# Decoder layer, up-projection by a seven-product scheme: two value buffers, norm weights moved from the weight tiles to the input's splits, sums of the first tile made in place in product order

## The chip, the cores and the metric

The kernel runs on one core of a Trainium2 chip. The metric is the device time of one execution in microseconds (us). The engines are TensorE (PE, with its weight loads as PEld), VectorE (DVE), ScalarE (ACT), GpSimd (POOL) and SyncE (SP, which here only issues DMAs). Each engine runs its own instructions in program order, and engines wait for one another on semaphores.

## What is computed

One layer of a hybrid decoder on 1040 prompt rows and 8 decode rows, all in float32. The change touches the end of the attention half (`h = x + mixed @ w_merge`) and the first half of the channel mixer:

```python
def rms_norm(x, w):
    y = xf * lax.rsqrt(jnp.mean(xf * xf, axis=-1, keepdims=True) + EPS)
    return (y * w.astype(jnp.float32)).astype(x.dtype)
...
    h = x + mixed @ w_merge
    hn = rms_norm(h, ffn_norm_w)
    g, val = jnp.split(hn @ w_up, [D_FF], axis=-1)
    g_hist = jnp.concatenate([ffn_prev.astype(x.dtype), g], axis=1)
    g_conv = causal_dwconv(g_hist, ffn_conv_w) + ffn_conv_b
    y = h + (jax.nn.silu(g_conv) * val) @ w_down
```

D_MODEL is 1024 and D_FF is 2816, so `w_up` is worked off in 22 tiles of 128 gate columns and 128 value columns.

## The kernel before

**Three products for one.** A float32 operand is split into a high part (ACT rounds a copy to float32r) and a low part (the rest, by a subtraction on DVE or POOL). Each product is high x high, high x low and low x high on TensorE.

**Seven products for eight.** For one tile of 128 gate and 128 value columns, `w_up` has four blocks of 512 x 128 (g1, g2, v1, v2) and the activations `h` have four blocks (upper or lower 512 features, first or second 520 columns). `sums` on DVE makes four sums of weight blocks (SW0 to SW3), and seven products P1 to P7 (24 matmuls of 260 columns each) stand for the eight block products. P1, P2 and P4 use g1, g2 and v2; P5, P6, P7 and P3 use SW0 to SW3. The activation side has B11 and B2 (blocks of `h`), T1, T2, T3 and T4 (their sums and differences), each with a high and a low part. These seven operands are made once, before and during the first tile, and serve all 22 tiles.

**One tile.** Tiles are numbered (i, a), a = 0 or 1; the loop runs over i, so two tiles per turn, and the first and the last ones are written out. After the first tile, TensorE takes the products in the order P1, P5, P6, P2, P7, P3, P4. P1, P6, P7 and P4 add up in one PSUM buffer (`MAIN[a]`), P2 stands in the other one, P5 and P3 in a third (`PXX`). After P1, P6, P5 and P4, ACT copies a half of a gate or value tile out of PSUM (copies G1, G2, V2, V1), and DVE adds the rest (adds G1, G2, V2). So P6 waits for copy G1, P7 for copy G2, P3 for copy V2, P4 for add V2, and the next tile's P1 and P5 for adds G1 and G2.

**What else goes on per tile.** DVE multiplies the two raw weight tiles by the norm weight (`scale`, twice), makes the four weight sums, multiplies the gate by the row norm RB (`gates`), does the width-3 convolution of the tile before (`conv`: two long instructions and three of 8 columns for the decode rows) and the last product with the value tile (`times_val`). ACT makes the high parts of the weights for the next tile (`high`), the first term of the convolution (`gate_half`), `silu`, and issues the store of the finished tile (`put_away`). POOL makes the low parts (`low`) and multiplies by the row norm (`times_rms`). SP loads the raw tiles RAWG and RAWV.

**One value buffer.** V serves all tiles. So copy V2 of a tile comes behind `put_away` of the tile before, and that waits for `times_val` on DVE, which reads the old V.

**The first tile** (`first_up` on TensorE, order P1, P2, P5, P3, P6, P7, P4) begins while its operands are still being made: DVE makes T3F, T2F, T4F for four feature groups kk after the merge is over, ACT rounds them, DVE makes the low parts of T2 and POOL those of T3 and T4. RB comes from a sum over rows on TensorE, three square roots on ACT and one `reciprocal` on DVE.

**Code order.** No scheduler is at work: each engine's order is the order in which its block is written. What the change moves is moved by hand.

Of the kernel before, what the change touches and what calls it, by code (L numbers as in the profile page):

```python
# [29 lines left out]
P = 128  # L30
# [13 lines left out]
YW = 344  # L44
# [50 lines left out]
def build(nc, io):  # L95
    ctx = ExitStack()
    with ctx:
# [116 lines left out]
        def parts(name, shape, high, low):  # L214
# [13 lines left out]
        T1F, T2F, T3F, T4F = (at(f"T{j}F", half, o) for j, o in (  # L228
            (1, oh1 + 3 * HB), (2, o7 + HB), (3, o7 + 3 * HB), (4, o7 + 5 * HB)))
# [5 lines left out]
        V = at("V", [P, NP], o1)  # L235
# [15 lines left out]
        HY = at("HY", [P, KD, NC], oh1 + 4 * HB)  # L251
# [118 lines left out]
        SUMS = {"P1": 1, "P2": 1, "P4": 2, "P5": 3, "P6": 4, "P7": 5, "P3": 6}  # L370
# [8 lines left out]
        def copied(i, a, what):  # L379

            order = ("G1", "V2", "G2", "V1") if is_first(i, a) else ("G1", "G2", "V2", "V1")
            return 22 + 4 * (2 * i + a) + order.index(what) + 1

        def added(i, a, what):

            return 21 + 3 * (2 * i + a) + ("G1", "V2", "G2").index(what) + 1

# [17 lines left out]
        def _(sp):  # L405
# [181 lines left out]

            sp.wait_ge(mm[1], place(NF // 2 - 1, 1, "P1"))
            activations(0, 0)
            down_weights(0)  # L590
            sp.wait_ge(mm[1], place(NF // 2 - 1, 1, "P7"))
            activations(1, 1)
            sp.wait_ge(mm[1], place(NF // 2 - 1, 1, "P3"))
            for m in range(KD):
                sp.dma_start(HY[:, m, :], hx_d[m, :, :]).then_inc(x_in[m], 16)
# [17 lines left out]
            for m in range(KD):  # L613
                sp.wait_ge(d_px, 24 * (NF // 2 - 1) + NCH * (m + 1))
                sp.dma_start(io["y"][:, m, :], HY[:, m, Y0:NC]).then_inc(out_done, 16)
# [7 lines left out]
        def _(pe):  # L623
# [424 lines left out]
            def first_up():  # L1048
# [10 lines left out]
                pe.wait_ge(n_rt, 5)  # L1059
# [10 lines left out]
                pe.wait_ge(n_lop, 12)  # L1070
# [51 lines left out]
        def _(act):  # L1122
# [413 lines left out]
            for m in range(8):  # L1536
                if m < 7:
                    hi(m % 2, 26 + m // 2)
                act.wait_ge(h_out, m + 1)
                if m >= 2:  # L1540
                    act.wait_ge(n_acc, KD + m - 2)
                nc.scalar.activation((HACC if m == 0 else HSQ)[:, :], HX[:, m, :], ACT.Square).then_inc(n_sq, 1)
                if m < 4:
                    nc.scalar.copy(B11[0][:, m, :], HX[:, m, 0:HALF]).then_inc(n_hi, 1)
                    act.wait_ge(n_t, KD + m + 1)
                    nc.scalar.copy(T1[0][:, m, :], T1F[:, m, :]).then_inc(n_hi, 1)
                else:
                    nc.scalar.copy(B2[0][:, m - 4, :], HX[:, m, :]).then_inc(n_hi, 1)
                act.dma_start(hx_d[m, :, :], HX[:, m, 0:NC]).then_inc(x_in[m], 16)
# [32 lines left out]
            def t_high(j, kk):  # L1582
                act.wait_ge(n_t, 12 + 3 * kk + (3, 2, 4).index(j) + 1)
                nc.scalar.copy((T2, T3, T4)[j - 2][0][:, kk, :], (T2F, T3F, T4F)[j - 2][:, kk, :]).then_inc(n_hi, 1)

            act.wait_ge(mm[0], 30)
            high(0, 0, "P5")
            copy(0, 0, "G1")
# [27 lines left out]
            def up(i, a, last=False):  # L1616
# [21 lines left out]
                copy(i, a, "V2")  # L1638
# [44 lines left out]
        def _(pool):  # L1683
# [187 lines left out]
            for p in ("P1", "P2", "P5", "P3"):  # L1871
                low(0, 0, p)
            for kk in range(4):
                t_low(3, kk)
# [605 lines left out]
```

## Time and profile before

| | us |
|---|---|
| median of 3 runs | 1815.49 (1811.84 to 1821.8) |
| the profiled execution | 1801.86 |
| its span | 1800.0 |
| end of the merge to first matmul of the up-projection | about 1032.5 to 1033.85 |
| up-projection's 22 tiles on TensorE | 1033.85 to about 1541 |
| down-projection | to the end |

The span is the time between the first and the last recorded instruction; the execution adds 1.86 us around it. The three timed runs lie 10 to 20 us above the profiled execution, so durations are read from the profile and the difference is put onto the median. A tile of the up-projection is found in the timeline by its matmuls on line 1043: `WP3H` is the weight of product P3, and so on.

### The profile page before, as it was taken

The page shows a single profiled execution, that of the slowest core. Times are in us where ns is not written, and L with a number is a line of the kernel's source. Part 1 is how long each engine was busy: PE and PEld are TensorE (multiplying, and loading weights), DVE is VectorE, ACT ScalarE, POOL GpSimd, SP SyncE. Part 2 cuts the span into 40 slices and gives each one's busy share as a digit, 9 for nine tenths or more (in the row PEclk, how much of TensorE's full clock was granted, in tenths as well). Part 3 has the DMA queues.
Part 4 walks back from the last instruction along what each step waited for, and adds up shares of the span by engine and source line. Part 5 has one row for each costly group of instructions (what it writes and reads, how often), then busy time and mean ns, then how long its engine had stood idle before and what let it go on. Part 6 is the DMA issues. An engine that isn't in the chain of part 4 may idle for free.

```text
span 1800.0 us, 32034 instructions
## 1 busy us (share of the span) xinstructions
PE 1689.1 (94%) x11519; PEld 1620.4 (90%) x11519; DVE 1303.0 (72%) x1988; ACT 687.3 (38%) x1049; POOL 902.2 (50%) x479
## 2 busy tenths in 40 slices
PE   7999999999999899998999968999999999999999
PEld 5868999999999798887999968999999999899999
DVE  5569999999899566555443398888888887555555
ACT  4755551322112477774112243333333334311110
POOL 2505751554876476662221267665666556544441
PEclk9999999999999799999999989999999999999999
DMA  5321112113775332222433212112222211622222
GB/s 192 85 64 36 47 40 91 56 51 116 255 229 193 106 89 83 83 95 83 137 123 141 98 56 71 70 70 71 73 76 77 75 72 62 244 94 94 94 75 94
DMA packets 66978, 178.32 MB, mean 99 GB/s; under 512 B 15386, under 2 KB 15514, under 8 KB 66762
## 3 DMA queue, kind: packets, MB, share of 16 engines
q1 hardware_dynamic: 56786, 140.91, 23.8%
q10 hardware_dynamic: 9392, 32.10, 4.7%
q0 software_dynamic: 720, 4.29, 0.6%
q8 instruction: 46, 0.75, 0.2%
q14 instruction: 34, 0.28, 0.1%
HBM read 141.79 MB, written 35.58 MB: 99 GB/s over the span
## 4 chain that ended last, share of the span: by engine, by line
PE 59%; DVE 24%; issue 7%; ACT 4%; POOL 3%; DMA 1%; SPq 1%; DVEq 1%; ACTq 1%; POOLq 0%
PE PS L634 16%; PE PX L1108 14%; PE PS L969 5%; PE PS L1014 4%; PE PX L1043 4%; PE PS L922 4%; DVE TG L2313 3%; DVE TG L2296 2%; PE PS L892 2%; DVE SW L2253 2%; DVE S L2067 2%; DVE M L2065 2%; PE PX L905 2%; PE PS L950 2%; DVE LD L2047 2%
## 5 line engine op out<-in xcount | busy, mean ns | idle before, releaser
L634 PE MATMUL PS<-XH,WHI 128*128 128x346 f32 (+1 forms) x984 | 321.2, 326 | 5.7 <-POOL WLO L1687 4.4
L634 PE MATMUL PS<-XL,WHI 128*128 128x346 f32 (+1 forms) x984 | 317.9, 323 | 0.0
L634 PE MATMUL PS<-XH,WLO 128*128 128x346 f32 (+1 forms) x984 | 317.3, 322 | 0.0
L1687 POOL TENSOR_TENSOR WLO<-WRAW,WHI 128x1024 fp32r<-128x1024 f32 x58 | 143.8, 2479 | 296.9 <-ACT WHI L1136 296.8
L2320 DVE TENSOR_TENSOR HY<-HY,PX 128x344 f32<-128x344 f32 x264 | 135.3, 513 | 114.0 <-PE PX L1108 114.0
L2067 DVE MATCH_REPLACE8 S<-M,S 128x1024 f32<-128x1024 f32 (+3 forms) x224 | 206.0, 926 | 0.0
L2065 DVE MAX8 M<-S 128x8 f32<-128x1024 f32 (+3 forms) x224 | 200.8, 932 | 0.4
L634 PEld LDWEIGHTS PS<-XH,WHI 128*128 128x128 f32 x984 | 186.4, 189 | 15.6 <-issue 8.9
L634 PEld LDWEIGHTS PS<-XH,WLO 128*128 128x128 f32 x984 | 186.5, 190 | 0.0
L634 PEld LDWEIGHTS PS<-XL,WHI 128*128 128x128 f32 x984 | 186.5, 189 | 0.0
L1108 PE MATMUL PX<-FH,DHI 128*128 128x344 f32 x528 | 169.5, 321 | 4.1 <-DVE HY L2320 4.1
L1108 PE MATMUL PX<-FH,DLO 128*128 128x344 f32 x528 | 169.4, 321 | 0.0
L1108 PE MATMUL PX<-FL,DHI 128*128 128x344 f32 x528 | 168.8, 320 | 0.0
L1785 POOL TENSOR_TENSOR RINGL<-RING,VH 128x512 fp32r<-128x512 f32 x64 | 82.0, 1281 | 78.8 <-ACT VH L1467 70.8
L1865 POOL TENSOR_TENSOR FL<-FRAW,FH 128x2064 fp32r<-128x2064 f32 x11 | 51.6, 4687 | 118.2 <-ACT FH L1653 118.2
L1108 PEld LDWEIGHTS PX<-FH,DHI 128*128 128x128 f32 x528 | 100.0, 189 | 4.8 <-DVE HY L2320 4.7
L1814 POOL TENSOR_TENSOR KR<-KR,QB 128x512 f32<-128x512 f32 x64 | 81.2, 1296 | 37.5 <-DMA KR<-cache_k 37.4
L1108 PEld LDWEIGHTS PX<-FL,DHI 128*128 128x128 f32 x528 | 99.7, 189 | 0.0
L1108 PEld LDWEIGHTS PX<-FH,DLO 128*128 128x128 f32 x528 | 99.5, 188 | 0.0
L1861 POOL TENSOR_TENSOR TG<-TG,RB 128x1032 f32<-128x1032 f32 x22 | 53.6, 2437 | 81.0 <-ACT TG L1574 81.0
L1043 PE MATMUL PX<-B2H,WP3H 128*128 128x260 f32 x176 | 52.9, 300 | 39.4 <-ACT V L1560 32.6
L922 PEld LDWEIGHTS PS<-VT,PTB 128*128 128x128 f32 (+1 forms) x704 | 82.6, 182 | 2.3 <-issue 0.2
(357 smaller groups left out, 5018.1 us busy)
## 6 DMA issues: line engine op xcount, KB each, us to landing
WRAW<-wtiles SPq DMA_DIRECT2D x49, 512.0 KB, 3.6
KR<-cache_k SPq DMA_DIRECT2D x64, 256.0 KB, 3.0
RING<-cache_v SPq DMA_DIRECT2D x64, 256.0 KB, 3.0
ffn_act<-TG ACTq DMA_DIRECT2D x22, 516.0 KB, 2.7
FRAW<-ffn_act SPq DMA_DIRECT2D x11, 1032.0 KB, 7.0
RAWG<-wtiles SPq DMA_DIRECT2D x22, 512.0 KB, 3.6
RAWV<-wtiles SPq DMA_DIRECT2D x22, 512.0 KB, 4.3
DRAW<-wdown SPq DMA_DIRECT2D x11, 1024.0 KB, 5.0
```

Source lines behind the costliest of these rows:

```text
L634: last = nc.tensor.matmul(PS[b][:, c, 0:n], w[b][:, kk, :], x[:, kk, t0 + c * n:t0 + (c + 1) * n], start=(kk == 0 and p == 0), stop=(kk == ...
L922: last = nc.tensor.matmul(px_out[u % 2][0:ROWS[b], :], PTB[u % 2][0:w, kt, 0:ROWS[b]], v, start=(kt == 0), stop=(kt == KT_N[b] - 1))
L969: last = nc.tensor.matmul(PS[q][:, c, 0:CW], w[b][:, 4 * q + kk, :], x[:, kk, C0 + c * CW:C0 + (c + 1) * CW], start=(kk == 0 and p == 0), ...
L1014: last = nc.tensor.matmul(PS[b][:, c, 0:n], w[b][:, kk, :], x[:, kk, t0 + c * n:t0 + (c + 1) * n], start=(kk == 0 and p == 0), stop=(kk == ...
L1043: last = nc.tensor.matmul(out[:, c, 0:HC], w[:, kk, :], x[:, kk, t0 + c * HC:t0 + (c + 1) * HC], start=new and kk == 0 and q == 0, stop=kk ...
L1108: last = nc.tensor.matmul(PX[q % 2][:, 0:YW], w[:, a, m * P:(m + 1) * P], x[:, a, c * YW:(c + 1) * YW], start=(a == 0 and p == 0), stop=(a ...
L1687: nc.gpsimd.tensor_tensor(WLO[b][:, :, :], WRAW[b][:, :, :], WHI[b][:, :, :].bitcast(F32), ALU.subtract).then_inc(w_lo[b], 1)
L1785: nc.gpsimd.tensor_tensor(RINGL[q // 8][:, q % 8, :], RING[q // 8][:, q % 8, :], VH[q % 8][:, :].bitcast(F32), ALU.subtract).then_inc(v_lo ...
L1814: nc.gpsimd.tensor_tensor(KR[KSLOT[g]][:, :], KR[KSLOT[g]][:, :], QB[s % 2][:, :], ALU.mult).then_inc(k_prod, 1)
L2065: ins = nc.vector.max(M8[x][0:ROWS[b], :], s)
L2067: ins = nc.vector.match_replace(s, M8[x][0:ROWS[b], :], s, TAKEN)
L2320: nc.vector.tensor_tensor(h, h, PX[q % 2][:, 0:YW], ALU.add).then_inc(d_px, 1)
```

## The change

Four things are done together.

1. **Two value buffers.** V becomes V[0] and V[1]. Copy V2 moves from behind `put_away` to right behind copy G1 on ACT, and the high part of P5 goes with it, ahead of `silu`. On POOL, the low part of P5 moves ahead of `times_rms`.
2. **Norm weights.** `scale` goes: the raw weight tiles are used as they are. The norm weight is multiplied into the activations: ACT's rounding of B11, T1 and B2 becomes an activation with a scale, DVE's low parts become `scalar_tensor_tensor`, and the four lower blocks of HX are multiplied in place during the merge (4 ACT instructions of 128x1040). On DVE, `sums` now comes ahead of `conv`.
3. **First tile.** T3, T2 and T4 are made in place in HX (`t_sums`), three of the four groups during the merge. Their high parts are rounded in the order of the products (all of T3, then T2, then T4), T4's low parts move from POOL to DVE, and a tiny square root behind the merge loads ACT's table ahead of time. `reciprocal` moves behind the sums for the second tile.
4. **Buffers.** WP3, WP4, WP7 and HY are put elsewhere, with waits that follow from it; two of the eight blocks of the residual are loaded back earlier.

```diff
-        V = at("V", [P, NP], o1)
...
+        V = [at("V0", [P, NP], om1 + 4 * NP), at("V1", [P, NP], orw + 12288)]
...
-            sp.wait_ge(n_t, 24)
-            sp.wait_ge(n_hi, 20)
-            sp.wait_ge(n_lo, 16)
-            for m in range(KD):
-                sp.wait_ge(x_in[m], 48)
+            sp.wait_ge(n_lo, 24)
+            sp.wait_ge(n_lop, 8)
             for which in range(2):
                 up_weights(0, 1, which)
...
-                pe.wait_ge(n_rt, 5)
+                pe.wait_ge(n_rt, 3)
                 product(0, 0, "P5")
...
-            for kk in range(2):
-                for j in (3, 2, 4):
-                    t_high(j, kk)
...
+            copy(0, 0, "G1")
+            act.wait_ge(n_acc, 2 * (KD - 1))
             high(0, 0, "P3")
+            t_high(3, 3)
+            for kk in range(4):
+                t_high(2, kk)
+            high(0, 0, "P6")
             copy(0, 0, "V2")
...
+            for kk in range(4):
+                t_high(4, kk)
+            act.wait_ge(n_lo, 24)
+            act.wait_ge(n_lop, 8)
+            high(0, 0, "P7")
+            high(0, 0, "P4")
             copy(0, 0, "G2")
...
                 copy(i, a, "G1")
                 if not last:
                     high(*then, "P1")
+                copy(i, a, "V2")
+                if not last:
+                    high(*then, "P5")
                 silu(j, b)
...
-                else:
-                    high(*then, "P5")
                 copy(i, a, "G2")
...
                 put_away(j, b)
-                copy(i, a, "V2")
...
                 low(*then, "P1")
+                low(*then, "P5")
                 times_rms(*preceding(i, a))
-                for p in AFTER[1:]:
+                for p in AFTER[2:]:
                     low(*then, p)
...
                 if not last:
-                    scale(*then, 0)
-                    scale(*then, 1)
-                conv(j, b)
-                if not last:
                     dve.wait_ge(w_lo[a], W0F[a] + 7 * i + 6)
                     sums(*then)
+                conv(j, b)
                 times_val(j, b)
```

**DVE, a tile of the loop.** Instructions of DVE in tile (0, 1), written out ahead of the loop and in the same order as in it, before the change. L2210 is `scale`, L2293 to L2306 are `conv`, L2248 to L2253 are `sums`, L2313 is `times_val`.

```order
L2210 TENSOR_TENSOR RAWG_195<-RAWG_195,WV 128x1024 [waits w_raw0]
L2210 TENSOR_TENSOR RAWV_197<-RAWV_197,WV 128x1024 [waits w_raw0]
L2293 SCALAR_TENSOR_TENSOR TG_193<-G_186,WV,TG_193 128x1032 [waits f_t0]
L2296 SCALAR_TENSOR_TENSOR TG_193<-G_186,WV,TG_193 128x1032 [waits f_s]
L2301 TENSOR_SCALAR TG_193<-WV 128x8 [waits f_s]
L2303 SCALAR_TENSOR_TENSOR TG_193<-WV,TG_193 128x8 [waits f_s]
L2306 SCALAR_TENSOR_TENSOR TG_193<-G_186,WV,TG_193 128x8 [waits f_s]
L2248 TENSOR_TENSOR SW_188<-RAWV_197 128x512 [waits u_s,w_lo1]
L2250 TENSOR_TENSOR SW_189<-SW_188,RAWG_195 128x512 [waits u_s]
L2251 TENSOR_TENSOR SW_190<-RAWG_195,RAWV_197 128x512
L2253 TENSOR_TENSOR SW_191<-RAWG_195,SW_189 128x512 [waits u_s]
L2313 TENSOR_TENSOR TG_193<-TG_193,V 128x1032 [waits ps_free0,f_rb]
```

The same place after the change:

```order
L2289 TENSOR_TENSOR SW_185<-RAWV_193 128x512 [waits w_raw0,w_lo1]
L2291 TENSOR_TENSOR SW_186<-SW_185,RAWG_191 128x512 [waits u_s]
L2292 TENSOR_TENSOR SW_187<-RAWG_191,RAWV_193 128x512
L2294 TENSOR_TENSOR SW_188<-RAWG_191,SW_186 128x512 [waits u_s]
L2324 SCALAR_TENSOR_TENSOR TG_189<-G_183,WV,TG_189 128x1032 [waits f_t0]
L2327 SCALAR_TENSOR_TENSOR TG_189<-G_183,WV,TG_189 128x1032 [waits f_s]
L2332 TENSOR_SCALAR TG_189<-WV 128x8 [waits f_s]
L2334 SCALAR_TENSOR_TENSOR TG_189<-WV,TG_189 128x8 [waits f_s]
L2337 SCALAR_TENSOR_TENSOR TG_189<-G_183,WV,TG_189 128x8 [waits f_s]
L2344 TENSOR_TENSOR TG_189<-TG_189,V_195 128x1032 [waits ps_free0,f_rb]
```

The two `scale` instructions are gone, and the four sums stand where they stood, ahead of the convolution.

**ACT, the same tile.** Before the change; L1567 and L1568 are `gate_half`, L1560 the copies out of PSUM, L1534 `high`, L1574 `silu`, L1580 the store of `put_away`.

```order
L1568 ACTIVATE TG_193<-G_186,WV 128x1032
L1560 COPY G_187<-PS 128x520 [waits mm1]
L1534 CAST WP1H<-RAWG_195 128x512 [waits mm1,u_s]
L1574 ACT_TABLE_LOAD
L1574 ACTIVATE TG_193<-TG_193,WV 128x1032 [waits f_cv]
L1534 CAST WP5H<-SW_188 128x512 [waits mm1,u_s]
L1560 COPY G_187<-PS 128x520 [waits mm1]
L1534 CAST WP6H<-SW_189 128x512 [waits mm1,u_s]
L1534 CAST WP2H<-RAWG_195 128x512 [waits mm1,u_s]
L1580 DMA ffn_act<-TG_193 128x1032 [waits f_a]
L1560 COPY V<-PX 128x520 [waits mm1]
```

And after it:

```order
L1599 ACTIVATE TG_189<-G_183,WV 128x1032
L1591 COPY G_184<-PS 128x520 [waits mm1]
L1559 CAST WP1H<-RAWG_191 128x512 [waits mm1,w_raw0]
L1591 COPY V_196<-PX 128x520 [waits mm1]
L1559 CAST WP5H<-SW_185 128x512 [waits mm1,u_s]
L1605 ACT_TABLE_LOAD
L1605 ACTIVATE TG_189<-TG_189,WV 128x1032 [waits f_cv]
L1591 COPY G_184<-PS 128x520 [waits mm1]
L1559 CAST WP6H<-SW_186 128x512 [waits mm1,u_s]
L1559 CAST WP2H<-RAWG_191 128x512 [waits mm1,w_raw0]
L1611 DMA ffn_act<-TG_189 128x1032 [waits f_a]
```

Copy V2 (`V<-PX`) has moved from behind the store, which waits for f_a, to behind copy G1; copy G2 (the second `G<-PS`) still stands behind `silu`.

**DVE, from the first tile to the second.** After the change (L2302 low parts of T2 and T4, L2313 the adds, L2318 `gates`); before it, RECIPROCAL stood right behind T2's low parts, ahead of the three adds.

```order
L2302 TENSOR_TENSOR T2L<-HX,T2H 128x520 [waits n_hi] x4
L2302 TENSOR_TENSOR T4L<-HX,T4H 128x520 [waits n_hi] x4
L2313 TENSOR_TENSOR G_183<-G_183,PS 128x520 [waits ps_free0,mm0]
L2313 TENSOR_TENSOR V_195<-V_195,PS 128x520 [waits ps_free0,mm0]
L2313 TENSOR_TENSOR G_183<-G_183,PX 128x520 [waits ps_free0,mm0]
L2289 TENSOR_TENSOR SW_185<-RAWV_194 128x512 [waits w_raw1,w_lo0]
L2291 TENSOR_TENSOR SW_186<-SW_185,RAWG_192 128x512 [waits u_s]
L2292 TENSOR_TENSOR SW_187<-RAWG_192,RAWV_194 128x512
L2294 TENSOR_TENSOR SW_188<-RAWG_192,SW_186 128x512 [waits u_s]
L2359 RECIPROCAL RB<-RB 128x1040 [waits n_rt]
L2318 TENSOR_TENSOR G_183<-G_183,RB 128x1040 [waits ps_free1,n_rc]
```

The reciprocal now stands between the sums for the second tile and the first tile's `gates`.

## Rows read from the trace of the kernel before

**Rows 1.** The page's busy times: us (share of the span) xinstructions.
```profile
PE 1689.1 (94%) x11519; PEld 1620.4 (90%) x11519; DVE 1303.0 (72%) x1988; ACT 687.3 (38%) x1049; POOL 902.2 (50%) x479
```

**Rows 2.** TensorE's timeline, first two tiles: start, duration, instruction [idle before, releaser].
```profile
1043.14 0.39 PE L1043 MATMUL PX<-T1H,WP5H 128*128 128x260 f32 x1 [1.57 <-ACT RB L1593]
1053.12 0.56 PE L1043 MATMUL PX<-B2H,WP3H 128*128 128x260 f32 x1 [6.83 <-POOL WP3L L1849]
...
1070.23 0.36 PE L1043 MATMUL PS<-T4H,WP4H 128*128 128x260 f32 x1 [2.98 <-POOL WP4L L1849]
...
1089.66 0.59 PE L1043 MATMUL PS<-T3H,WP7H 128*128 128x260 f32 x1 [4.68 <-ACT G L1560]
```

**Rows 3.** TensorE's waits, 1100 to 1520: us in total, times, longest.
```profile
PE PX L1043 <- ACT V L1560: 31.6, 19, 1.8
```

**Rows 4.** The chain that ended last: start, us, engine and line.
```profile
1095.09 3.17 PE PX L1043 x24
...
1515.20 3.15 PE PX L1043 x24
1518.35 5.78 PE PS L1043 x48
...
1535.66 2.88 PE PX L1043 x24
```

**Rows 5.** Stretches: length, busy us (x) of PE, PEld, DVE, ACT, POOL, then granted clock.
```profile
1050.00:1055.00 5.00, 1.88 (x9) 1.91 (x10) 3.31 (x5) 4.46 (x9) 3.76 (x3) 0.50 0.59 210
...
1090.00:1095.00 5.00, 4.12 (x24) 3.91 (x23) 4.63 (x3) 1.20 (x4) 5.00 (x3) 0.74 0.12 49
```

**Rows 6.** DVE's timeline in one tile of the loop.
```profile
1209.18 0.69 DVE L2281 TENSOR_TENSOR G<-G,PX 128x520 f32<-128x520 f32 x1 [2.67 <-PE PX L1043]
1209.90 2.26 DVE L2287 TENSOR_TENSOR G<-G,RB 128x1040 f32<-128x1040 f32 x1
...
1213.22 2.31 DVE L2210 TENSOR_TENSOR RAWV<-RAWV,WV 128x1024 f32<-128x1024 f32 x1
...
1220.74 0.69 DVE L2250 TENSOR_TENSOR SW<-SW,RAWG 128x512 f32<-128x512 f32 x1
...
1226.64 0.68 DVE L2281 TENSOR_TENSOR G<-G,PS 128x520 f32<-128x520 f32 x1
```

**Rows 7.** POOL's timeline in the same tile.
```profile
1209.78 1.28 POOL L1849 TENSOR_TENSOR WP3L<-SW,WP3H 128x512 fp32r<-128x512 f32 x1 [1.50 <-ACT WP3H L1534]
1213.16 1.29 POOL L1849 TENSOR_TENSOR WP4L<-RAWV,WP4H 128x512 fp32r<-128x512 f32 x1 [2.09 <-ACT WP4H L1534]
...
1225.59 2.26 POOL L1849 TENSOR_TENSOR WP6L<-SW,WP6H 128x512 fp32r<-128x512 f32 x1
```

**Rows 8.** ACT's timeline in the same tile.
```profile
1220.24 1.16 ACT L1574 ACTIVATE TG<-TG,WV 128x1032 f32<-128x1032 f32 x1 [4.28 <-DVE TG L2306]
...
1221.81 0.59 ACT L1560 COPY G<-PS 128x520 f32<-128x520 f32 x1
...
1227.27 0.59 ACT L1560 COPY V<-PX 128x520 f32<-128x520 f32 x1 [3.08 <-DVE TG L2313]
```

**Rows 9.** Instructions of the tile TG: duration in ns min/median/max, first and last start.
```profile
L2296 DVE SCALAR_TENSOR_TENSOR TG<-G,WV,TG x22: 1294/2094/2222, 1081.6 to 1544.6; 128x1032 f32<-128x1032 f32 x22
...
L2303 DVE SCALAR_TENSOR_TENSOR TG<-WV,TG x22: 225/227/1180, 1085.0 to 1546.2; 128x8 f32<-128x8 f32 x22
...
L2313 DVE TENSOR_TENSOR TG<-TG,V x22: 1226/2338/2345, 1091.7 to 1555.8; 128x1032 f32<-128x1032 f32 x22
```

**Rows 10.** Timelines of DVE, POOL and ACT, merge's end and first tile.
```profile
1022.37 1.07 ACT L1542 ACTIVATE HSQ<-HX 128x1040 f32<-128x1040 f32 x1 [8.44 <-DVE HX L2221]
...
1055.18 6.64 DVE L2270 RECIPROCAL RB<-RB 128x1040 f32<-128x1040 f32 x1
...
1040.37 1.28 ACT L1590 ACT_TABLE_LOAD   x1
...
1052.94 6.00 POOL L1857 TENSOR_TENSOR T3L<-T3F,T3H 128x520 fp32r<-128x520 f32 x4
```

More of the change, by code:

```diff
@@ L379, in copied, with b11_high, t1_high, scaled @@
         def copied(i, a, what):
-            order = ("G1", "V2", "G2", "V1") if is_first(i, a) else ("G1", "G2", "V2", "V1")
-            return 22 + 4 * (2 * i + a) + order.index(what) + 1
+            return 22 + 4 * (2 * i + a) + ("G1", "V2", "G2", "V1").index(what) + 1
         def added(i, a, what):
             return 21 + 3 * (2 * i + a) + ("G1", "V2", "G2").index(what) + 1
+        def b11_high(m):
+            return KD + 3 * m + 1
+        def t1_high(m):
+            return KD + 3 * m + 2
+        def scaled(m):
+            return KD + 3 * m + 3
+        def b2_high(m):
+            return KD + 12 + m - 3
+        def t_split(j, kk):
+            return 24 + 4 * (3, 2, 4).index(j) + kk + 1
+        def t_summed(j, kk):
+            return KD + 4 + 3 * kk + (3, 2, 4).index(j) + 1
         def following(i, a):
@@ L593, in _ @@
             sp.wait_ge(mm[1], place(NF // 2 - 1, 1, "P3"))
-            for m in range(KD):
-                sp.dma_start(HY[:, m, :], hx_d[m, :, :]).then_inc(x_in[m], 16)
+            for m in range(2, KD):
+                residual_back(m)
             sp.wait_ge(d_lo, 1)
@@ L1538, in _ @@
                     hi(m % 2, 26 + m // 2)
+                if 1 <= m < 5:
+                    act.wait_ge(x_in[m - 1], 48)
+                    act.wait_ge(n_lo, 4 + 2 * m)
+                    nc.scalar.activation(HX[:, m - 1, :], HX[:, m - 1, :], ACT.Copy,
+                                         scale=WV[:, W_FN + m - 1:W_FN + m]).then_inc(n_hi, 1)
                 act.wait_ge(h_out, m + 1)
@@ L1582, in t_high @@
             def t_high(j, kk):
-                act.wait_ge(n_t, 12 + 3 * kk + (3, 2, 4).index(j) + 1)
-                nc.scalar.copy((T2, T3, T4)[j - 2][0][:, kk, :], (T2F, T3F, T4F)[j - 2][:, kk, :]).then_inc(n_hi, 1)
+                act.wait_ge(n_t, t_summed(j, kk))
+                nc.scalar.copy({2: T2, 3: T3, 4: T4}[j][0][:, kk, :], TF[j][:, kk, :]).then_inc(n_hi, 1)
+            nc.scalar.activation(M8[0][:, 0:1], eps, ACT.Sqrt)
             act.wait_ge(mm[0], 30)
+            for kk in range(3):
+                t_high(3, kk)
             high(0, 0, "P5")
-            copy(0, 0, "G1")
             act.wait_ge(n_sum, 2)
@@ L1869, in weight_low @@
                 nc.gpsimd.tensor_tensor(DLO[b][:, :, :], DRAW[:, :, :], DHI[b][:, :, :].bitcast(F32), ALU.subtract).then_inc(d_lo, 1)
[L1871 to L1874, printed above, removed]
+            low(0, 0, "P1")
+            low(0, 0, "P2")
+            t_low(0)
+            low(0, 0, "P5")
+            t_low(1)
+            t_low(2)
+            low(0, 0, "P3")
+            t_low(3)
             low(0, 0, "P6")
             low(0, 0, "P7")
-            for kk in range(4):
-                t_low(4, kk)
             low(0, 0, "P4")
@@ L2343, in up @@
                 add(i, a, "V2")
+                add(i, a, "G2")
                 gates(i, a)
```

137 lines of the change are left out of this document (68 added, 69 removed).

## Prediction

> **What bounds the kernel now.** I read the head of the page first. TensorE is busy 94% of the span [rows 1], so a gain can only come out of the few per cent in which it waits, and I looked for those. In the timeline of TensorE the attention half and the down-projection show nothing that this change touches; the gaps that it can touch lie in two places.
>
> The first is the beginning of the up-projection. In the first two tiles TensorE waits 1.57, 6.83, 2.98 and 4.68 us [rows 2] (two smaller gaps aside). They also cost clock: the granted clock is 0.50 from 1050 to 1055 and 0.74 from 1090 to 1095 [rows 5], so matmuls right behind the two long gaps ran partly at 1.2 GHz and not at 2.4. I put that at 3 us, from half a stretch of 5 us lost at 0.74 and 0.50. Together 19 us.
>
> The second is the steady loop. The waits of TensorE hold only one line for tiles 2 to 20: product P3 waits for copy V2, 31.6 us in 19 waits [rows 3]. The chain gives the period: P3 of tile 1 starts at 1095.09, that of tile 20 at 1515.20, so 420.11 us in 19 tiles, 22.11 us each [rows 4]. The last tile has no such wait and takes 20.46 us from P3 to P3, with two products in 5.78 us, 2.89 each [rows 4]. Seven of these are 20.2 us. So 1.9 us of each of 19 tiles is there to be had, 36 us at most: 1.66 us of wait, and about 0.26 us because a product that starts out of a wait takes 3.15 us and not 2.89 [rows 4].
>
> **The chains that take over.** Removing one wait helps as far as the next one. In the loop, copy V2 starts at 1227.27, behind `times_val` and the store [rows 8]; it could have started when P5 was done, some 9 us earlier. With two buffers, and the copy ahead of `silu`, that wait goes. Next comes copy G2, for which P7 waits and which still stands behind `silu`. Its chain is: P3 ends, add G2, `gates`, (two `scale`), `conv`, `silu`, copy G2, P7. In the tile of the rows, P3's last matmul issues at about 1208.8, just ahead of add G2 at 1209.18 [rows 6]. P4, P1, P5, P6 and P2 follow with no gap, 5 times 2.89, so P7 can start at 1223.25. Copy G2 ends at 1221.81 + 0.59 = 1222.4 [rows 8]. Slack 0.85 us. That is little, so what the change does to this chain decides.
>
> **What blocks DVE.** `gates` takes 2.26 us at 1209.90 while POOL's WP3L runs to 1211.06; `scale` takes 2.31 us at 1213.22 while WP4L runs to 1214.45 [rows 6, 7]. In both, DVE ends 1.1 us after POOL does: an instruction of DVE with two inputs in SBUF stands still until POOL's is done. The reverse holds too: WP6L, issued at 1225.59, takes 2.26 us and not 1.29, behind `times_val`. Yet add G1, with an input in PSUM, takes 0.68 us at 1226.64 in the middle of WP6L [rows 6, 7]. So each pair of DVE and POOL instructions that meet costs up to 1.3 us.
>
> **The loop, step by step,** on the same clock. `gates` ends at 1212.16 as before. Removed: two `scale`, which filled the time to conv's start at about 1215.45. In their place now stand the four sums. Each takes 0.69 us alone [rows 6], 2.75 together; WP4L at 1213.16 blocks one of them for about 1 us, so conv starts at 1215.9. Its first instruction runs 1.29 us (the minimum of its second one [rows 9]) to 1217.2. WP1L then has POOL's turn, 1.3 us, and the second instruction ends at 1219.55 (its median of 2.09 us is this same meeting, as it is now [rows 9]). New is WP5L: P5 ends at 1208.8 + 3 x 2.89 = 1217.5, copy V2 and the high part take 0.6 each, so it asks at 1218.9, starts when DVE is done, and runs to 1220.85. The three small instructions of conv, 0.23 us each alone, wait for it: one of them took 1.18 us where it met POOL [rows 9]. conv ends at 1221.6, against 1220.1 now (`silu` starts at 1220.24 [rows 8]). Then `silu` 1.16 us and copy G2 at once (before, WP5H stood between them, 0.5 us): the copy ends at 1223.4. P7 starts at 1223.5, a gap of 0.25 us. From P3's end to P3's end that is 14.7 us, 3.15 for P7 out of a wait, and 2.89 for P3: **20.7 us per tile, against 22.11; 19 tiles give 26.8 us.**
>
> Two checks on the others. Add V2 must be done before P4: `silu` ends at 1222.95, `times_rms` about 2 us later, then `times_val` behind one block (2.34 [rows 9]), adds G1 and V2 0.7 each: 1228.8, while P4 can start at 1229.5. Slack 0.7 us. ACT's pointer scales and the in-place multiplication fall in the merge, where ACT waits 8.44 us for its next input [rows 10], so they cost nothing; without that cover the four instructions of 1.1 us would cost 4.5 us. The scaled forms of DVE's low parts run at about a column per ns (1.29 us for 1032 [rows 9]), as the subtractions do.
>
> **The first two tiles.** The square roots lose the table load of 1.28 us [rows 10] ahead of them, and P5 waits for one of them and not three: the wait of 1.57 us goes, P5 runs from 1041.5 to 1044.4. P3 waits for copy V2, which on ACT stands behind WP3H, one T3H, four T2H and WP6H. Their inputs are the four sums and three instructions of `t_sums` on DVE, while POOL makes T3's low parts (6.00 us for four [rows 10]) and WP5L. If no instructions meet, copy V2 is done at 1045.9, if each meets one, at 1049.9: a gap of 1.5 to 5.5, not 6.83. P7 waits for copy G2, now behind T4's low parts on DVE: 0.9 to 1.7. P4 waits for add V2 directly behind P7: 0.9. The wait of 2.98 for WP4L goes, since POOL no longer makes T4's low parts.
>
> Then something gets worse. The reciprocal of 6.64 us ran before the change from 1055.18, while TensorE was waiting anyway [rows 10]; now it stands ahead of `gates` of tile 0. From P7's end: add V2 and add G2 1.4, sums 2.8, reciprocal 6.64, `gates` 1.2, `gate_half` and copy G1 of tile 1 2.0: 14.1 us, while TensorE has P4, P1 and P5, 9.6 us with the 0.9. So P6 of tile 1 waits 4.5 us, and P7 behind conv and `silu` another 1.4 to 4. Sum 9.2 to 16.6, in the middle 13, less than half of it in one gap; one gap of 4 to 5 us costs clock as before, about 1. Against 19 that is **a gain of 5 us, with the small gaps 7** (bounds 2 and 12).
>
> Here the Trainium skill would say something else of the table: "ScalarE: Activation LUTs", section What ACT_TABLE_LOAD costs, gives 1.283 us for the load and 1.38 for a drain, 2.66 together. The trace does not agree: the first square root starts as the load's 1.28 us end. By the page 1.4 us more would be gained.
>
> **Sum.** 26.8 + 7 = 34 us. The profiled execution took 1801.86 us, so 1768. The median of the runs lies 13.6 us above it, and I take the same distance: **1781 us.**
>
> **Rivals.**
> - *TensorE becomes the bound* (0.15). DVE and POOL fall into another rhythm in which WP5L does not meet the small instructions. Copy G2 is then back before 1223.25. Period 20.2, gain 36, and the start at its better bound 12: 1815.5 − 48 = 1767. For it: the gap that I forecast is 0.25 us. Against it: every late low part meets something.
> - *The wait moves from P3 to P7* (0.15). One more meeting of 1.29 us on the chain, and the period is 22.0. Gain 2 plus 7: 1806. For it: the slack was only 0.85 us, and conv is later than before by my own count.
> - *Slower* (0.05). Two more meetings put 2.6 us on the chain from P3's end to P7: period 23.3, 19 tiles lose 22.6, the start gives back 7: 1831. It decides from a chain 2 us longer than I count (19 times 0.6 over 22.11 eats the 7 and 4 more). For it: three of POOL's seven low parts now fall between `gates` and `silu`, where two did. Against it: each can stop DVE only once, and I have counted all three.
>
> The rule behind the second and the third stands in the Trainium skill, "SBUF — State Buffer", section SBUF: two separate sides: VectorE and GpSimd share one pair of ports as an exclusive lock, and the loser is blocked for the whole instruction. The trace agrees: `gates` ends 1.1 us behind WP3L.
>
> **How the numbers follow.** Chances: forecast 0.65 (period 20.4 to 21.3, start 2 to 12: a gain of 17 to 44), rivals 0.15, 0.15 and 0.05. A measurement here tells about 0.5%, 9 us. The forecast and the first rival are faster, the second is on the edge (half of it), so faster 0.87, same 0.08, slower 0.05. The range takes in the first rival and the better half of the second: 1763 to 1800.
>
> **What would show it.** P3's waits for copy V2 gone; `conv` ending 12.8 us after P3's end; P7 waiting 0.1 to 0.5 us for copy G2 in each tile, at a granted clock of 1.00; periods of 20.4 to 21.0 us; a gap of about 4.5 us at P6 of tile 1; the down-projection unchanged. The forecast is wrong if P7 waits a microsecond or more, if P4 waits for add V2, or if the gaps of the first two tiles add up to more than 16 us.

## The result, and the profile after

The changed kernel takes 1766.93 us (median of 4 runs, 1765.94 to 1768.72) against 1816.97 (1811.84 to 1821.8) before: a ratio of 0.9726, 95% interval 0.9697 to 0.9755. It is faster, as forecast, and by more than the 34 us that I had summed: the medians lie 50.0 us apart. The two profiled executions, 1801.86 and 1766.9, lie 34.9 apart. That 34.9 meets my 34 is a coincidence, and so it is read by stages below.

The head of the changed kernel's page, busy time of each engine; [rows 1] is its counterpart.

```profile
PE 1689.7 (96%) x11519; PEld 1625.3 (92%) x11519; DVE 1239.7 (70%) x1948; ACT 694.5 (39%) x1054; POOL 893.8 (51%) x475
```

TensorE does the same work in a shorter span. Its timeline in the changed kernel, the rows at which it had been idle (start, duration, instruction, [idle before, releaser]), and P7 and P3 of tiles without a wait; [rows 2] and [rows 4] answer to it.

```profile
1053.44 0.39 PE L1065 MATMUL PX<-B2H,WP3H 128*128 128x260 f32 x1 [2.85 <-ACT V L1591]
1062.30 0.36 PE L1065 MATMUL PS<-T3H,WP7H 128*128 128x260 f32 x1 [1.32 <-POOL WP7L L1881]
1066.20 0.39 PE L1065 MATMUL PS<-T4H,WP4H 128*128 128x260 f32 x1 [0.79 <-DVE V L2313]
1079.76 0.58 PE L1065 MATMUL PS<-T2H,WP6H 128*128 128x260 f32 x1 [4.64 <-ACT G L1591]
1088.73 0.39 PE L1065 MATMUL PS<-T3H,WP7H 128*128 128x260 f32 x1 [0.68 <-ACT G L1591]
1091.72 0.28 PE L1065 MATMUL PX<-B2H,WP3H 128*128 128x260 f32 x1
...
1230.13 0.28 PE L1065 MATMUL PS<-T3H,WP7H 128*128 128x260 f32 x1
...
1495.25 0.28 PE L1065 MATMUL PX<-B2H,WP3H 128*128 128x260 f32 x1
...
1507.39 0.42 PE L1130 MATMUL PX<-FH,DHI 128*128 128x344 f32 x1 [4.04 <-DVE HY L2351]
1520.98 0.42 PE L1130 MATMUL PX<-FH,DHI 128*128 128x344 f32 x1 [3.28 <-DVE HY L2351]
```

Stretches of the changed kernel: length, TensorE's busy time (instructions), granted clock, DMA share, GB/s.

```profile
1080.00:1085.00 5.00, 5.00 (x24) 0.51 0.65 211
...
1095.00:1490.00 395.00, 395.00 (x3292) 1.00 0.22 78
```

From P3 of tile 1 to P3 of the last one it takes 403.53 us, 20.18 a tile, where the kernel before took 440.57 [rows 4]. The clock of 0.51 (near 1.2 GHz) stands right behind the gap of 4.64 us at P6 of tile 1. In 395 us of the loop TensorE is busy for 395, at a clock of 1.00 (2.4 GHz): no product waits for anything. That is my first rival, TensorE as the bound, and not the gap of 0.25 us at P7 that I forecast.

The stages of all kernels, worked out from the starts of rows like those above (P1 of tile 0, P3 of tile 1, first and last matmul of FH and DHI in the down-projection). The experiments are explained below.

| kernel | first P1 at | P1 to P3 of tile 1 | to the down-projection | down, first to last | median us |
|---|---|---|---|---|---|
| before (the profile shown) | 1033.85 | 61.24 | 446.2 | 254.5 | 1816.97 |
| before, run again | 1044.05 | 62.03 | 446.4 | 261.0 | 1816.59 |
| changed | 1039.63 | 52.09 | 409.5 | 259.6 | 1766.93 |
| changed, run again | 1041.45 | 52.08 | 409.6 | 259.6 | 1768.02 |
| multiplications kept | 1040.03 | 55.64 | 420.4 | 259.6 | 1782.77 |
| copy V2 late | 1040.97 | 53.08 | 434.5 | 258.0 | 1791.41 |
| longer chain | 1039.52 | 53.05 | 436.9 | 259.3 | 1794.88 |
| sums late | 1040.03 | 58.62 | 409.4 | 258.0 | 1776.3 |
| reciprocal cut | 1040.66 | 53.54 | 409.7 | 259.4 | 1768.65 |
| conv first | 1043.65 | 51.31 | 409.4 | 258.0 | 1767.76 |
| tail on POOL | 1044.02 | 52.06 | 409.4 | 254.5 | 1765.36 |
| reciprocal cut, tail on POOL | 1040.93 | 53.61 | 409.7 | 254.3 | 1763.7 |
| all three | 1041.64 | 49.23 | 410.3 | 254.4 | 1760.0 |

One of the six timed runs of "reciprocal cut, tail on POOL" took 2350.65 us at a granted clock of 0.65; it counts in that median, which is 1762.79 without it. "Longer chain" is a single run.

So from profile to profile: loop 37 us less, start 9.1 less, but the attention half 5.8 more and the down-projection 5.1 more.

### The profile page after: what moved, and what is told of

Read it like the earlier page. It is cut to its first block, busy times and chain, and to the rows that moved or that the text cites. A ratio compares the mean times of both kernels' runs of the same rounds, so it can differ in the third digit from the quotient of the medians.

```text
span 1765.1 us, 31960 instructions
## 1 busy us (share of the span) xinstructions
PE 1689.7 (96%) x11519; PEld 1625.3 (92%) x11519; DVE 1239.7 (70%) x1948; ACT 694.5 (39%) x1054; POOL 893.8 (51%) x475
## 4 chain that ended last, share of the span: by engine, by line
PE 77%; DVE 10%; ACT 3%; issue 3%; SPq 3%; POOL 2%; DMA 1%; ACTq 0%; DVEq 0%; POOLq 0%
PE PS L1065 17%; PE PS L656 16%; PE PX L1130 14%; PE PX L1065 7%; PE PS L991 5%; PE PS L1036 5%; PE PS L944 3%; PE PS L914 2%; DVE S L2100 2%; DVE M L2098 2%; PE PS L972 2%; PE PX L927 2%; DVE LD L2080 2%; PE PS L759 1%; DMA KR<-cache_k 1%
## 5 line engine op out<-in xcount | busy, mean ns | idle before, releaser
L2344 DVE TENSOR_TENSOR TG<-TG,V 128x1032 f32<-128x1032 f32 x22 | 50.2, 2283 | 73.6 <-POOL TG L1891 73.6
L1685 ACT CAST FH<-FRAW 128x2064 fp32r<-128x2064 f32 x10 | 19.2, 1923 | 174.4 <-PE PX L1130 173.1
```

## The experiments

**The kernel before, run again.** No edit. The question is whether the 5.8 and the 5.1 us belong to the change.

> The kernel before, once more, with a profile of its own. The medians of before and after differ by 50.0 us, the two profiled executions only by 34.9. Theory: the first half of the program, ahead of the up-projection, takes a different time from execution to execution; then the first matmul of the up-projection starts 5 to 20 us off 1033.85, and the loop's period is 22.1 us as before. Rival: the loop itself is slower in other executions, because its waits sometimes cost clock; then the period is 22.4 us or more and the start of the up-projection is within 2 us of 1033.85.

Median 1816.59 over ten runs (1811.55 to 1821.77), ratio 1.0002 (0.9979 to 1.0026). The profiled execution took 1819.63, and its first P1 stands at 1044.05, 10.2 us later than in the profile shown. The theory holds: the first matmul lies 10 us off, and the loop's period is 22.0 us. One stretch of the attention half, first in the profile shown and then in this one (columns as above):

```profile
700.00:800.00 100.00, 95.74 (x746) 0.97 0.29 81
```

```profile
700.00:800.00 100.00, 95.98 (x734) 0.93 0.29 85
```

The same program is granted 0.97 in one execution and 0.93 in the other. The second place was a surprise: the beginning of the down-projection, from TensorE's, DVE's and POOL's timelines of the kernel before, run again.

```profile
1573.68 0.43 PE L1108 MATMUL PX<-FH,DHI 128*128 128x344 f32 x1 [3.90 <-DVE HY L2320]
```

```profile
1568.38 4.83 DVE L2313 TENSOR_TENSOR TG<-TG,V 128x1032 f32<-128x1032 f32 x1
```

```profile
1567.45 4.67 POOL L1869 TENSOR_TENSOR DLO<-DRAW,DHI 128x2048 fp32r<-128x2048 f32 x1 [1.67 <-ACT DHI L1660]
```

The last `times_val` (1.23 us at the least [rows 9]) comes 0.9 us behind the start of POOL's low part of the second down weights, and ends 1.1 us behind its end. DVE's adds queue behind it, and TensorE waits 3.90 us for them. In the profile shown it started at 1555.8 and was free, so there the down-projection took 254.5 us and here 261.0. The profile shown was thus an unusually quick execution in two places, 10.2 + 6.5 us, nearly all of the 17.8 by which the spans differ (1817.8 and 1800.0). So the meeting in the down-projection is not new with the change. In the kernel before it went either way: POOL's low part started 0.8 us behind `times_val` in the profile shown and 0.9 ahead of it here. In the changed kernel it starts 1.5 us ahead (1514.76 and 1516.28); whether the change makes the meeting more frequent, two profiles of the kernel before cannot show.

**The multiplications kept.** The changed kernel, with two multiplications by ones of the raw tiles on DVE, in its old order.

```diff
...
                 if not last:
+                    scale(*then, 0)
+                    scale(*then, 1)
+                conv(j, b)
+                if not last:
                     dve.wait_ge(w_lo[a], W0F[a] + 7 * i + 6)
                     sums(*then)
-                conv(j, b)
```

> The changed kernel with the two multiplications of each raw weight tile put back on DVE (by ones instead of the norm weight, from tile 1 on), and DVE's old order: multiplications, convolution, sums. So the loop holds the two value buffers alone. Theory: the wait for copy V2 was the only bound, the multiplications were covered; copy G2 comes at most 0.3 us late, the period is 20.2 to 20.6 us, and the time 2 to 10 us above the changed kernel, 2.5 of it at the first tile. Rival: DVE's work per tile was a bound of its own, and taking the multiplications out brought a good part of the gain; then the period is 21 us or more, and the time 18 us or more above the changed kernel.

1782.77 (1777.01 to 1786.05), 15.8 us above the changed kernel, between the two expectations: the loop gives back 10.9 us and the start 3.6. TensorE's timeline of this kernel in one tile:

```profile
1306.13 0.40 PE L1065 MATMUL PS<-T4H,WP4H 128*128 128x260 f32 x1 [0.22 <-DVE V L2323]
```

Now P4 waits for add V2, in 18 tiles of the loop and for 4.3 us in all. So the multiplications were not all covered: half a microsecond a tile of the loop's gain is owed to their going and to the new order of `sums` and `conv`, which no run takes apart.

**Copy V2 late.** The changed kernel, with the old order on ACT and POOL; the second buffer stays.

```diff
-                copy(i, a, "V2")
-                if not last:
-                    high(*then, "P5")
                 silu(j, b)
...
+                else:
+                    high(*then, "P5")
                 copy(i, a, "G2")
...
                 put_away(j, b)
+                copy(i, a, "V2")
...
```

> The changed kernel with ACT's and POOL's old order in the loop: copy V2 again behind the store of the tile before, the high part of P5 behind the activation, the low part of P5 behind the multiplication by the row norm. The weights stay unscaled. Theory: P3 waits for copy V2 again, 1.0 to 1.7 us a tile, the period is 21.4 to 22.0 us and the time 24 to 36 us above the changed kernel. Rival: the lighter DVE alone brings the stored tile early enough; then the period is 20.2 to 20.6 us.

1791.41 (1790.56 to 1792.71), 24.5 us above the changed kernel; the loop alone is 25.0 longer. TensorE's longest entry among the waits of this kernel (us in total, times, longest), as in [rows 3]:

```profile
PE PX L1066 <- ACT V L1592: 24.3, 21, 2.8
```

The longest of these 21 waits, 2.8 us, is that of tile 0, which the changed kernel has too; the loop's are the other 20, 21.4 us. The theory holds: with the second buffer but in the old order, the wait is back. The copy has to leave its place behind the store, and the second buffer is what lets it. Its 25.0 us and the 10.9 of the multiplications with DVE's order make up nearly all of the loop's 36.9 (446.4 less 409.5).

**A longer chain.** The changed kernel with one more multiplication of the gate by ones behind `gates`, to learn what is next in line.

```diff
...
+                dve.wait_ge(f_g, 2 * (2 * i + a) + 1)
+                nc.vector.tensor_tensor(G[a][:, :], G[a][:, :], CK[:, C_ONES:C_ONES + 1].to_broadcast([P, NP]),
+                                        ALU.mult).then_inc(f_g, 1)
```

> The changed kernel with one more instruction of DVE in each tile: the gate tile is multiplied by ones behind the multiplication by the row norm, 128x1040, 1.24 us alone, up to 2.3 where it meets POOL. Nothing else of the program changes. Theory: the chain from the end of P3 over the gates, sums, convolution, activation and copy G2 to P7 is next in line, with 0.35 us to spare; then P7 waits 0.8 to 1.9 us in each tile for copy G2, and the period is 21.1 to 22.3 us. Rival: the chain has more room than that; then P7 does not wait and the period stays at 20.2 us.

1794.88 in one run. The waits of this kernel:

```profile
PE PS L1065 <- ACT G L1591: 29.6, 21, 6.8
```

The longest of these, 6.8 us, is P6 of tile 1 with copy G1. The other 20 are P7 with copy G2, one in each of tiles 1 to 20, 22.7 us in all. The chain that I had named was the right one, and the changed kernel stands just below the point from which it decides.

**Sums late.** The changed kernel with all four `t_sums` behind the merge.

```diff
-                    if m < 7:
-                        t_sums(m - 4)
...
-            t_sums(3)
+            for kk in range(4):
+                t_sums(kk)
```

> The changed kernel with all four groups of t_sums behind the merge and not one of four. Theory (the gain of 9.0 us at the start comes from the sums made during the merge): nine more DVE instructions of 0.6 to 1.8 us stand ahead of P3 and P7 of the first tile, so the start loses 6 to 9 us: 1773 to 1776. Rival (the start gained from the order of the roundings and of the low parts, not from the early sums): within 2 us of the changed kernel, 1765 to 1769.

1776.3 (1772.2 to 1778.99), 9.4 us above; the start takes 58.62 us and not 52.09, so 6.5 of them are the start's. TensorE's timeline of this kernel, P5 of tile 0:

```profile
1055.02 0.56 PE L1065 MATMUL PX<-T1H,WP5H 128*128 128x260 f32 x1 [7.26 <-POOL WP5L L1881]
```

Where the changed kernel does not wait at P5, this one waits 7.26 us: of the start's gain of 9.1 us the sums during the merge are the larger part. What the order of the roundings, the table load and the going of `scale` bring of the rest is not taken apart.

**The reciprocal cut.** In the changed kernel DVE is idle for 4.7 us ahead of add V2 of tile 0 and then runs the reciprocal for 6.65; here 680 of its 1040 columns go ahead of that add, and 360 stay (not 368, as the expectation says).

```diff
             add(0, 0, "G1")
+            dve.wait_ge(n_rt, 5)
+            nc.vector.reciprocal(RB[:, 0:680], RB[:, 0:680]).then_inc(n_rc, 1)
             add(0, 0, "V2")
...
-            nc.vector.reciprocal(RB[:, :], RB[:, :]).then_inc(n_rc, 1)
-            dve.wait_ge(n_rc, 3)
+            nc.vector.reciprocal(RB[:, 680:NP], RB[:, 680:NP]).then_inc(n_rc, 1)
+            dve.wait_ge(n_rc, 4)
...
```

> The changed kernel with the reciprocal cut in two: columns 0 to 679 right behind add G1 of tile 0, where DVE was idle for 4.68 us, and the other 368 behind the sums for the second tile. Theory (the 6.65 us of the reciprocal ahead of the gates of tile 0 make the gap of 4.64 us at P6 of tile 1, and the clock of 0.51 right behind it): some 4.3 us of it move into DVE's idle time, the gap at P6 of tile 1 falls under 1 us, no low clock behind it, P1 to P3 of tile 1 takes 46 to 49 us and not 52.25, and the kernel is 4 to 6 us faster than the changed one: about 1761 to 1763. Rival (what TensorE doesn't wait for at P6 it waits for at P7 of tile 1, behind conv and silu): the gap moves by one product and less than 2 us are gained: 1765 to 1767.

1768.65 (1766.76 to 1770.91): nothing gained, the rival. Timelines of this kernel, TensorE in tile 1 and then DVE:

```profile
1077.07 0.39 PE L1065 MATMUL PS<-T2H,WP6H 128*128 128x260 f32 x1 [0.92 <-ACT G L1591]
...
1089.73 0.59 PE L1065 MATMUL PS<-T3H,WP7H 128*128 128x260 f32 x1 [6.63 <-ACT G L1591]
```

```profile
1061.70 4.39 DVE L2355 RECIPROCAL RB<-RB 128x680 f32<-128x680 f32 x1
...
1070.46 2.39 DVE L2360 RECIPROCAL RB<-RB 128x360 f32<-128x360 f32 x1
...
1078.92 1.76 DVE L2289 TENSOR_TENSOR SW<-RAWV 128x512 f32<-128x512 f32 x1 [3.67 <-POOL WP3L L1881]
...
1084.61 1.28 DVE L2324 SCALAR_TENSOR_TENSOR TG<-G,WV,TG 128x1032 f32<-128x1032 f32 x1
```

The cut does what it should, and the gap at P6 falls from 4.64 to 0.92 us. But the sums for the third tile, which now come ahead of conv, wait 3.67 us for POOL to be done with the old ones, and conv, `silu` and copy G2 stand behind them. The whole wait comes back at P7.

**Conv first.** The changed kernel, reciprocal whole, with conv of tile 0 ahead of those sums, and ACT's high part of P5 behind `silu` and copy G2 in that tile.

```diff
...
+                first = isinstance(i, int) and i == 0
+                if first:
+                    conv(j, b)
                 if not last:
                     dve.wait_ge(w_lo[a], W0F[a] + 7 * i + 6)
                     sums(*then)
-                conv(j, b)
+                if not first:
+                    conv(j, b)
```

> The changed kernel with conv of tile 0 ahead of the sums for the third tile, not behind them, and on ACT the high part of P5 for the third tile behind silu; the reciprocal whole. Theory (P6 of tile 1 waits for gates behind the reciprocal, and only from there on conv's place counts): the gap at P6 stays 4.6 us, the gap of 0.68 at P7 goes, from the first matmul to P3 of tile 1 51 to 52 us. Rival (conv's place is what makes both gaps): the gap at P6 shrinks and the stage takes under 50 us.

1767.76 (1763.87 to 1768.93); the start takes 51.31 us. TensorE's timeline of this kernel:

```profile
1083.77 0.58 PE L1065 MATMUL PS<-T2H,WP6H 128*128 128x260 f32 x1 [4.63 <-ACT G L1591]
```

The theory holds: the gap at P6 is the reciprocal's, and stays, and the one of 0.68 us at P7 is gone. Neither edit alone gains anything worth a measurement.

**The tail on POOL.** The changed kernel with the last tile's `times_val` on POOL.

```diff
...
+            nc.gpsimd.tensor_tensor(TG[1][:, :], TG[1][:, :], V[1][:, Y0:NC], ALU.mult).then_inc(f_a, 1)
...
-                if m == 2:
-                    times_val(NF // 2 - 1, 1)
```

> The changed kernel with the last tile's product with the value tile on POOL instead of DVE. Theory (this product on DVE, 4.21 us and not 1.23, meets DVE's adds of the down-projection and POOL's low part of the first down weights, which makes the gap of 3.28 us in TensorE and the low clock behind it): gap under 1 us, the down-projection's matmuls back from 240.5 to about 239 us, 3.5 to 5.5 us faster than the changed kernel: about 1762 to 1763. Rival (POOL gets to the low parts of the second down weights and of the activations later, and TensorE waits for these): the gap moves, and the kernel is within 1.5 us of the changed one.

1765.36 (1761.55 to 1766.14). DVE's and POOL's timelines of the changed kernel at the place in question, and then POOL's of this one:

```profile
1516.28 4.21 DVE L2344 TENSOR_TENSOR TG<-TG,V 128x1032 f32<-128x1032 f32 x1
```

```profile
1514.76 4.64 POOL L1899 TENSOR_TENSOR DLO<-DRAW,DHI 128x2048 fp32r<-128x2048 f32 x1
```

```profile
1512.45 2.02 POOL L1891 TENSOR_TENSOR TG<-TG,RB 128x1032 f32<-128x1032 f32 x1 [7.11 <-ACT TG L1605]
1514.55 2.02 POOL L1937 TENSOR_TENSOR TG<-TG,V 128x1032 f32<-128x1032 f32 x1
1516.52 4.66 POOL L1895 TENSOR_TENSOR FL<-FRAW,FH 128x2064 fp32r<-128x2064 f32 x1
```

The low part that `times_val` meets is that of the second down weights, not of the first as the expectation says. The gap of 3.28 us is gone, and the down-projection takes 254.5 us and not 259.6, as the theory has it. The medians show only 1.6 of these 5.1 us, which is outside the theory's 3.5 to 5.5. In the profiled execution, 0.8 us shorter than the changed kernel's, the first P1 came 4.4 us later; that the other executions lost the gain in the same way is not shown.

**Reciprocal cut and tail on POOL.**

> Both of these edits at once: reciprocal cut in two, and the last tile's product with the value tile on POOL. They lie at the two ends of the up-projection, so by the theory their gains add up: 8 to 11 us faster than the changed kernel, 1756 to 1759, a ratio of about 0.967 to the kernel before. If both rivals hold, 1764 to 1767.

1763.7, ratio 0.9712 (0.9666 to 0.9758). The tail's 5.3 us are there; the start's are not, for the reason just shown.

**The changed kernel, run again.** No edit; on the same chip as the kernel that follows.

> The changed kernel once more, unaltered. Theory (the attention half shifts from one execution to the next and the stages behind it don't): the first matmul of the up-projection starts anywhere between 1034 and 1045, but from there to P3 of tile 1 it takes 52.1 us again, with the gap of 4.6 us at P6 of tile 1, and from the first to the last start of a down matmul 259.6 us with the gap of about 3.3 us. Rival (the stages shift too): those two times differ by more than 1 us, and the times by stage of the two runs before tell nothing.

1768.02 (1765.91 to 1768.91), stages 52.08, 409.6 and 259.6: within 0.1 us of the first profile, while the first P1 came 1.8 us later. The stages stand still and the attention half shifts, so for a few microseconds I compare stages.

**All three.** Reciprocal cut, conv first, tail on POOL; the edits are those above.

> Reciprocal cut in two, conv of tile 0 ahead of the sums with the high part of P5 behind silu, and the last tile's product with the value tile on POOL. With the reciprocal cut alone, P7 of tile 1 waits 6.6 us, because DVE's sums for the third tile stand 3.67 us waiting for POOL's WP3L with conv behind them. Theory: conv fits into that idle time, copy G2 of tile 1 is done about 1 us before P7 asks, the gap of 6.6 us and the low clock behind it (0.63 and 0.69) go, so from the first matmul to P3 of tile 1 45 to 47 us, against 53.6 with the cut alone and 52.1 in the changed kernel; with the 5 us at the down-projection the kernel is about 1756, 10 to 12 us faster than the changed one. Rival (the next wait in line takes the place: P3 of tile 1 for copy V2, or P1 of the third tile): 50 to 53 us, and 1760 to 1764.

1760.0 (1754.79 to 1762.32), ratio 0.9687 (0.966 to 0.9714). All five runs lie below all four of the changed kernel on the same chip; the medians are 8.0 us apart. Timelines of this kernel, TensorE in tile 1 and then DVE:

```profile
1078.06 0.40 PE L1065 MATMUL PS<-T2H,WP6H 128*128 128x260 f32 x1 [0.92 <-ACT G L1591]
...
1086.37 0.39 PE L1065 MATMUL PS<-T3H,WP7H 128*128 128x260 f32 x1 [2.26 <-ACT G L1591]
```

```profile
1077.57 2.15 DVE L2331 SCALAR_TENSOR_TENSOR TG<-G,WV,TG 128x1032 f32<-128x1032 f32 x1 [1.32 <-ACT TG L1599]
1079.75 2.21 DVE L2334 SCALAR_TENSOR_TENSOR TG<-G,WV,TG 128x1032 f32<-128x1032 f32 x1
1082.00 1.14 DVE L2339 TENSOR_SCALAR TG<-WV 128x8 f32<-128x8 f32 x1
1083.18 1.20 DVE L2341 SCALAR_TENSOR_TENSOR TG<-WV,TG 128x8 f32<-128x8 f32 x1
```

The start takes 49.23 us: 2.85 better than the changed kernel, 4.4 better than the cut without conv's move, and short of the 45 to 47 of the theory. P7 still waits 2.26 us, because conv, moved into DVE's idle time, ran beside four of POOL's low parts there: the four rows take 6.70 us, where undisturbed ones take 1.28, 1.29, 0.23 and 0.23, 3.03 in all. DVE was idle, but POOL was not. The granted clock is 0.72 from 1085 to 1090, behind that wait.

## Why the prediction came out as it did

**The wait removed: right.** The 31.6 us of P3's waits for copy V2 are gone, and putting the copy back brings 21.4 of them back.

**The chain that takes over: right chain, its length 0.4 us too long; the step that failed.** "P7 starts at 1223.5, a gap of 0.25 us": counted from the start of add G2 [rows 6], I had the copy done after 14.2 us, while TensorE gets to P7 after 14.1. The same tile in the changed kernel, in the timelines of DVE, ACT and POOL; [rows 6 to 8] answer to them.

```profile
1216.00 0.70 DVE L2313 TENSOR_TENSOR G<-G,PX 128x520 f32<-128x520 f32 x1 [1.29 <-PE PX L1065]
1216.73 2.35 DVE L2318 TENSOR_TENSOR G<-G,RB 128x1040 f32<-128x1040 f32 x1
...
1220.33 1.79 DVE L2292 TENSOR_TENSOR SW<-RAWG,RAWV 128x512 f32<-128x512 f32 x1
...
1222.64 1.28 DVE L2324 SCALAR_TENSOR_TENSOR TG<-G,WV,TG 128x1032 f32<-128x1032 f32 x1
1224.07 2.10 DVE L2327 SCALAR_TENSOR_TENSOR TG<-G,WV,TG 128x1032 f32<-128x1032 f32 x1
1226.43 0.94 DVE L2332 TENSOR_SCALAR TG<-WV 128x8 f32 x1 [0.26 <-DVE TG L2327]
...
1227.77 0.23 DVE L2337 SCALAR_TENSOR_TENSOR TG<-G,WV,TG 128x8 f32<-128x8 f32 x1
```

```profile
1224.55 0.59 ACT L1591 COPY V<-PX 128x520 f32<-128x520 f32 x1 [1.76 <-PE PX L1065]
...
1228.13 1.16 ACT L1605 ACTIVATE TG<-TG,WV 128x1032 f32<-128x1032 f32 x1 [2.47 <-DVE TG L2337]
1229.20 0.57 ACT L1591 COPY G<-PS 128x520 f32<-128x520 f32 x1
```

```profile
1219.99 1.58 POOL L1881 TENSOR_TENSOR WP4L<-RAWV,WP4H 128x512 fp32r<-128x512 f32 x1 [2.00 <-ACT WP4H L1559]
1222.87 2.21 POOL L1881 TENSOR_TENSOR WP1L<-RAWG,WP1H 128x512 fp32r<-128x512 f32 x1 [1.29 <-ACT WP1H L1559]
1225.75 1.59 POOL L1881 TENSOR_TENSOR WP5L<-SW,WP5H 128x512 fp32r<-128x512 f32 x1 [0.67 <-ACT WP5H L1559]
```

All three meetings that I counted are there: one sum of 1.79 us with WP4L, conv's second instruction with WP1L, its first small one with WP5L. conv starts 6.64 us behind add G2 (6.7 forecast), and its second instruction ends after 10.17 (10.4). No one term is far off; four come out about 0.1 us shorter each: the time to conv's start, conv's two long instructions, WP5L behind them (it ends after 11.34 us, where I had 11.7) and the small ones. So conv ends 12.0 us behind add G2 and not 12.4, and the copy is done at 1229.77, 13.8 us behind. P7 stands at 1230.13 and never waits: slack 0.36. Crossing that point saves the gap and the slower start of a product out of a wait with it, so 0.4 us of chain became 0.53 us of period, 20.18 and not 20.7, or 10.2 us in all. I gave that outcome 0.15 as a rival, with a period of 20.2; by a margin of 0.25 us out of 14, which was less than the uncertainty of any one meeting, it should have had as much as the forecast. The longer chain confirms that this wait is the next in line. Behind it comes P4 with add V2, from DVE's timeline of the changed kernel:

```profile
1234.26 0.68 DVE L2313 TENSOR_TENSOR V<-V,PS 128x520 f32<-128x520 f32 x1
```

The add is done 0.95 us before P4 starts at 1235.89, where I had a slack of 0.7.

The Trainium skill, "SBUF — State Buffer", section SBUF: two separate sides, has it that the loser of the lock between VectorE and GpSimd is blocked for the whole instruction. The trace of the changed kernel agrees: the last `times_val` ends at 1520.49, 1.1 us behind the end of POOL's 4.64 us.

**Norm weights: more than nothing.** I took the multiplications as filled-in time whose place the sums take. Put back, in DVE's old order, they cost the loop 10.9 us and the start 3.6.

**The start: right.** 9.1 us gained where I had 7 (2 to 12). P5's wait is gone; P3 waits 2.85 (1.5 to 5.5 forecast), P7 1.32 (0.9 to 1.7), P4 0.79 (0.9), P6 of tile 1 4.64 (4.5), P7 of tile 1 0.68, where I had 1.4 to 4. The clock of 0.51 stands behind the one long gap.

**The down-projection unchanged: open.** It took 5.1 us longer than in the profile shown, and 1.4 less than in the kernel before, run again.

**The offset of 13.6 us: it stood, and the 34 us were too few.** The median before does lie 13.6 us above the profile shown, because that execution was quick in two places; the changed kernel's median lies on its profile. Between the medians the change gains 50.0 us where I had 34, and that is the miss of 14.1 us between 1781 and 1766.93. Most of it is the loop's gain, put 10.2 us too low, and the start's, put 2.1 too low. That the sum without the offset, 1768, meets the changed kernel's profiled 1766.9 is luck: there these 12.3 us are offset by the 5.8 and 5.1 of the two stages in which the profile before was quick. Against the kernel before, run again, the changed kernel's profile is 52.7 us shorter in span: 36.9 in the loop, 9.9 in the start, 1.4 in the down-projection, 4.4 ahead of the up-projection. The last does not come out of the merge, where the change begins: from the merge's first matmul (at 952.38 and 962.55 before, 958.16 and 959.95 in the changed kernel's two profiles) to the first P1 all four take 81.5 us. What lies ahead of the merge shifts from execution to execution, by 10.2 us between the two profiles before.

## What to carry to other kernels

Where a chain that takes over misses the busy engine's time by less than one instruction's uncertainty, give both outcomes like chances: the period snaps to that engine's own time once the wait is gone. Moving work into an engine's idle time gained nothing here while conv stood behind the next wait in order, and less than counted where POOL, beside which DVE's instructions get longer, was busy at that time. One profile of the kernel before is one execution: where the timed runs lie 1% above it, profile stages again before a sum is made against it.

## What the runs showed of the hardware

The kernel before spread from 1800.87 to 1824.98 us over all its runs, with a granted clock of 0.97 in one and 0.93 in another execution of the same 100 us of attention, while the up-projection's stages repeated within a microsecond. An 8-column instruction of DVE, 0.23 us alone, takes 0.94 to 1.20 beside POOL's low parts. Where DVE and POOL both have work queued, both get longer, not one alone: a sum of 1.79 us and not 0.69 beside a WP4L of 1.58 and not 1.29.
